# Normalization tile by tile in a fused seven-sublayer transformer kernel: x updated straight from PSUM, squares and sums placed among the products, h made and awaited per tile

## The reference

```python
h = x * rsqrt(mean(x * x, axis=-1) + 1e-6) * gain     # first block: h = h * (1 + scale) + shift
x = x + gate * sublayer(h)                            # second block: gate 1, no shift
```

## Time and profile before

| | us |
|---|---|
| median of 3 runs (range) | 3588.69 (3579.77 to 3588.9) |
| the profiled execution's own time | 3586.82 |
| its span, first to last instruction | 3584.4 |
| PE busy | 3003.4 (84%) |
| DVE busy | 2309.0 (64%) |
| ACT busy | 1371.9 (38%) |
| mean granted PE clock | 0.921 of full speed |

### The profile page before, as it was taken

One profiled execution on the slowest core, in us unless ns is written; L12 is line 12 of the kernel. 1 busy time (PEld: TensorE's weight loads), 2 busy tenths in 40 slices (PEclk: granted clock), 3 DMA queues, 4 the chain that ended last, 5 costly groups with the idle time before them and its releaser, 6 DMA issues.

```text
span 3584.4 us, 48021 instructions
## 1 busy us (share of the span) xinstructions
PE 3003.4 (84%) x18518; PEld 2646.4 (74%) x18518; DVE 2309.0 (64%) x3078; ACT 1371.9 (38%) x1347; POOL 498.3 (14%) x244
## 2 busy tenths in 40 slices
PE   1987537978986569855799999999877999999998
PEld 1776326867775558644699999888666999998887
DVE  5985555867645746445489787556554797874565
ACT  1433223434435134322344443444333444344443
POOL 0420001302200002000078100000000582000000
PEclk9999758989998789876899999999988999999999
DMA  6985204776543025420345566567543455665675
GB/s 232 344 277 177 78 0 147 268 241 229 205 158 117 0 98 185 152 71 1 132 166 184 200 217 216 189 240 283 203 141 111 166 181 189 224 221 188 238 275 201
DMA packets 146097, 640.20 MB, mean 179 GB/s; under 512 B 12057, under 2 KB 45889, under 8 KB 89409
## 3 DMA queue, kind: packets, MB, share of 16 engines
q1 hardware_dynamic: 127584, 572.12, 46.2%
q10 hardware_dynamic: 18400, 66.59, 5.1%
HBM read 604.04 MB, written 34.62 MB: 178 GB/s over the span
## 4 chain that ended last, share of the span: by engine, by line
PE 75%; DVE 14%; ACT 4%; DMA 4%; issue 3%; POOL 0%; DVEq 0%; SPq 0%; ACTq 0%
PE pp L436 19%; PE pp L438 10%; PE pp L547 7%; PE pp L548 7%; PE pp L549 7%; PE mz L614 6%; PE mz L616 6%; PE mz L617 6%; PE mz L590 2%; DVE ada_raw L1017 2%; PE mz L428 2%; DVE gsq L1078 2%; DMA ada_raw<-ada 1%; DVE w_lo L988 1%; ACT w_hi L737 1%
## 5 line engine op out<-in xcount | busy, mean ns | idle before, releaser
L988 DVE TENSOR_TENSOR w_lo<-raw,w_hi 128x2048 fp32r<-128x2048 f32 (+1 forms) x422 | 923.9, 2190 | 482.3 <-ACT w_hi L737 481.4
L737 ACT ACTIVATE w_hi<-raw 128x2048 fp32r<-128x2048 f32 (+1 forms) x486 | 894.5, 1841 | 511.2 <-DMA raw<-expert_v 366.1
L436 PE MATMUL pp<-hs,w_hi 128*128 128x512 f32 x2400 | 863.0, 404 | 123.2 <-DVE hs L1037 116.7
L438 PE MATMUL pp<-hs,w_lo 128*128 128x256 f32 x2400 | 678.5, 283 | 0.0
L436 PEld LDWEIGHTS pp<-hs,w_hi 128*128 128x128 f32 x2400 | 459.1, 191 | 243.6 <-DVE hs L1037 120.7
L547 PE MATMUL pp<-hs,w_hi 128*128 128x256 f32 x2048 | 584.8, 286 | 0.0
L548 PE MATMUL pp<-hs,w_hi 128*128 128x256 f32 x2048 | 579.3, 283 | 0.0
L549 PE MATMUL pp<-hs,w_lo 128*128 128x256 f32 x2048 | 579.1, 283 | 0.0
L1506 POOL TENSOR_TENSOR w_lo<-raw,w_hi 128x2048 fp32r<-128x2048 f32 x64 | 319.2, 4999 | 1224.3 <-ACT w_hi L737 1224.3
L438 PEld LDWEIGHTS pp<-hs,w_lo 128*128 128x128 f32 x2400 | 461.1, 192 | 0.0
L436 PE MATMUL pp<-us,w_hi 128*128 128x512 f32 x960 | 351.8, 409 | 107.2 <-DVE us L1089 74.5
(11 more groups left out here) (245 smaller groups left out, 3219.9 us busy)
## 6 DMA issues: line engine op xcount, KB each, us to landing
raw<-expert_u SPq DMA_DIRECT2D x128, 1024.0 KB, 4.9
raw<-expert_v SPq DMA_DIRECT2D x128, 1024.0 KB, 4.9
raw<-ffn_in SPq DMA_DIRECT2D x88, 1024.0 KB, 4.9
raw<-ffn_down SPq DMA_DIRECT2D x64, 704.0 KB, 4.1
ada_raw<-ada ACTq DMA_DIRECT2D x76, 512.0 KB, 5.4
ada_raw<-ada ACTq DMA_DIRECT2D x22, 1024.0 KB, 6.3
raw<-out_w SPq DMA_DIRECT2D x16, 1024.0 KB, 4.9
raw<-hgrn SPq DMA_DIRECT2D x16, 1024.0 KB, 4.9
```

Of the source, the lines that this page charges most:

```text
L436: mm(outp, w_hi[:, slot, a:a + P], rhs[:, k0 + k].rearrange("p a t -> p (a t)"), start=(k0 + k == 0), stop=False, skip_group_check=True)
L438: last = mm(outp[:, 0:T], w_lo[:, slot, a:a + P], rhs[:, k0 + k, 0, :], start=False, stop=(k0 + k == last_k), skip_group_check=True)
L737: f(w_hi[:, slot, 0:n], raw[:, slot, 0:n], ACT.Copy).then_inc(hi_ready, 1)
L988: v.tensor_tensor(w_lo[:, slot, 0:n], raw[:, slot, 0:n], w_hi[:, slot, 0:n].bitcast(F32), ALU.subtract)\
```

## The change

- **x from PSUM.** `ffn_down` and `out_product` have no cross copy and no `add_halves`. DVE does two multiply-adds per tile straight from PSUM (first half, a wait on itself, second half), and `x_done` counts tiles (8 per sublayer). PE waits for `x_done` where it waited for `evac_done`.
- **Squares and sums among the products.** ACT squares one or two tiles as soon as they are updated, from within its `ffn_down` and `out_product` loops; PE's sums stand between products. After `ffn_down` rows, seven of the eight sums stand before or within the last row; in `out_product`, two after the third chunk and two after the fourth.
- **Root.** ACT does a one-column Sqrt before the last squares, so that a table load falls there.
- **h per tile.** DVE computes `x * gain * inv_rms` per tile, ACT makes the high part with the shift as bias, DVE the low part; PE waits per tile in the first output tile of the next phase.
- **u per tile.** PE waits for 11 tiles of u at the first `ffn_down` product and then per tile.
- **After PEER.** `y_tok` is copied by ACT and DVE in four parts, transposes release x two tiles at a time, x is added in four steps. The output goes out in four transfers.
- `h32` moves to where `cross` and `both` lie, `sq` to a free region; ACT's wait for `hs_ready` (L783) goes, and so does its wait for `ada_read` before the first norm (L914).

```diff
@@ memory
+        h32 = at("h32", [P, KD, T], F32, M)
+        sq = at("sq", [P, KD, T], F32, B)
@@ SP
-            sp.wait_ge(x_done, NORMS)
-            sp.dma_start(out, xT[:]).then_inc(out_done, 16)
+            for b in range(4):
+                sp.wait_ge(x_done, KD * (NORMS - 1) + 2 * b + 2)
+                sp.dma_start(out[:, 2 * b:2 * b + 2], xT[:, 2 * b:2 * b + 2]).then_inc(out_done, 16)
@@ PE
+            def sums(n, a, b):
+
+                for k in range(a, b):
+                    pe.wait_ge(norm_sq, KD * n + k + 1)
+                    last = mm(mz[:, 0, 0:T], ones, sq[:, k, :], start=(k == 0), stop=(k == KD - 1), skip_group_check=True)
+                if b == KD:
+                    last.then_inc(norm_sum, 1)
...
+                def tile_of_h(k):
+                    pe.wait_ge(hs_ready, KD * n + k + 1)
...
-                pe.wait_ge(u_lo, KF * (q + 1))
                 pe.wait_ge(evac_done, ph.evac0)
-                for rp, pair, half, lap in pairs_of(pe, ph):
-                    pe.wait_ge(evac_done, ph.evac0 + rp - 1)
+
+                def tile_of_u(k):
+                    if k == 0 or k >= KF // 2:
+                        pe.wait_ge(u_lo, KF * q + max(k + 1, KF // 2))
+
+                for rp, pair, half, lap in itertools.chain(pairs_of(pe, ph.part(0, 2)), pairs_of(pe, ph.part(2, KD - 2))):
+                    if not isinstance(rp, int) or rp > 1:
+                        pe.wait_ge(x_done, KD * n + rp - 1)
                     for j in range(2):
                         pe.wait_ge(lo_ready, 2 * pair + j + 1)
+                        first = isinstance(rp, int) and rp == 0
+                        if isinstance(rp, int) and rp == KD - 1:
+                            sums(n + 1, *((0, 6), (6, 7))[j])
...
+                sums(n + 1, KD - 1, KD)
@@ PE out_product
+                        if c > 1:
+                            pe.wait_ge(x_done, KD * n + 2 * c - 2)
+                        for t in range(2):
+                            last = tile_product(pp[:, j, t], 2 * half + j, t * KD, us, 0, KD, KD - 1)
+                        last.then_inc(w_used, 1)
+                        if c > 1:
+                            sums(n + 1, 2 * c - 4, 2 * c - 2)
+                sums(n + 1, KD - 4, KD)
@@ ACT
+            def squares(n, a, w):
+
+                act.wait_ge(x_done, KD * (n - 1) + a + w) if n else act.wait_ge(x_in, 16)
+                f(sq[:, bass.ds(a, w)], xT[:, bass.ds(a, w)], ACT.Square).then_inc(norm_sq, w)
+
+            def norm(n, a):
+
+                f(small[:, 63:64], eps, ACT.Sqrt)
+                for k in range(a, KD, 2):
+                    squares(n, k, min(2, KD - k))
                 act.wait_ge(norm_sum, n + 1)
                 f(inv_rms[:], mz[:, 0, 0:T], ACT.Sqrt, bias=eps, scale=1.0 / D).then_inc(norm_rms, 1)
-                act.wait_ge(norm_h, n + 1)
-                f(hs[:, :, 0, :], h32[:], ACT.Copy).then_inc(norm_hi, 1)
-                if n in (0, 2, 3):
-                    act.wait_ge(hs_ready, n + 1)
+                for k in range(KD):
+                    act.wait_ge(norm_h, KD * n + k + 1)
+                    f(hs[:, k, 0, :], h32[:, k], ACT.Identity, bias=a_add[:, n, k:k + 1]).then_inc(norm_hi, 1)
@@ ACT ffn_down
                     for j in range(2):
                         split_next(ph, rp, pair, half, lap, j)
                         load_modulation(ph, 2 * rp + j + 1, 1 - j)
-                    take_cross(ph, ph.evac0 + rp, half, 2 * pair + 2, 1)
+                        if j == 0 and not (isinstance(rp, int) and rp == 0):
+                            squares(n + 1, rp - 1, 1)
@@ DVE
-                link(v.tensor_tensor(h32[:], xT[:], inv_rms[:].unsqueeze(1).to_broadcast([P, KD, T]), ALU.mult))
-                for k in range(KD):
-                    last = v.tensor_scalar(h32[:, k], h32[:, k], a_mul[:, n, k:k + 1], a_add[:, n, k:k + 1], ALU.mult, ALU.add)
-                last.then_inc(norm_h, 1)
-                dve.wait_ge(norm_hi, n + 1)
-                v.tensor_tensor(hs[:, :, 1, :], h32[:], hs[:, :, 0, :].bitcast(F32), ALU.subtract).then_inc(hs_ready, 1)
+                for k in range(KD + 1):
+                    if k < KD:
+                        v.scalar_tensor_tensor(h32[:, k], xT[:, k], a_mul[:, n, k:k + 1], inv_rms[:], ALU.mult, ALU.mult).then_inc(norm_h, 1)
+                    if k:
+                        dve.wait_ge(norm_hi, KD * n + k)
+                        v.scalar_tensor_tensor(hs[:, k - 1, 1, :], h32[:, k - 1], a_add[:, n, k - 1:k],
+                                               hs[:, k - 1, 0, :].bitcast(F32), ALU.add, ALU.subtract).then_inc(hs_ready, 1)
+
+            def add_to_x(ps, g, xk, done):
+
+                v.scalar_tensor_tensor(xk, ps[0], g, xk, ALU.mult, ALU.add).then_inc(x_half, 1)
+                dve.wait_ge(x_half, done + 1)
+                v.scalar_tensor_tensor(xk, ps[1], g, xk, ALU.mult, ALU.add).then_inc(x_done, 1)
@@ DVE after PEER
-                dve.wait_ge(y_mm, l + 1)
-                v.tensor_tensor(xT[:].rearrange("p k t -> p (k t)"), xT[:].rearrange("p k t -> p (k t)"),
-                                pp.rearrange("p a b n -> p (a b n)"), ALU.add).then_inc(x_done, 1)
+                dve.wait_ge(w_used, 2 * (ph.pair0 + ph.pairs))
+                for dh in range(2):
+                    v.tensor_copy(y_tok[:, 1, dh * 512:(dh + 1) * 512], mz[:, 2 + dh]).then_inc(y_cp1, 1)
+                for b in range(4):
+                    dve.wait_ge(y_mm, 4 * l + b + 1)
+                    xb_ = xT[:, 2 * b:2 * b + 2].rearrange("p k t -> p (k t)")
+                    v.tensor_tensor(xb_, xb_, pp[:, b // 2, b % 2], ALU.add).then_inc(x_done, 2)
```

More of the change, by code:

```diff
@@ L17 @@
+import itertools
 import math
@@ L528, in attention, with out_product @@
                 weigh(HEADS - 1)
-            def out_product(i):
+            def out_product(i, n):
                 pe.wait_ge(mix_lo, i + 1)
-                products(plan[("out", i)], us)
+                ph = plan[("out", i)]
+                for rp, pair, half, lap in each_pair(ph):
+                    for j in range(2):
+                        c = 2 * rp + j
+                        pe.wait_ge(lo_ready, 2 * pair + j + 1)
+                        if c > 1:
[6 more added lines that the diff above has]
+                sums(n + 1, KD - 4, KD)
             def up(ph, q, spread=None, fresh=False):
@@ L631, in _ @@
             pe.wait_ge(evac_done, 1)
[L633 to L635 removed]
+            sums(0, 0, KD)
+            ffn(0, 0)
             ph = plan[("attn", 0)]
[L637 removed]
+            products(ph, 1)
             pe.wait_ge(evac_done, ph.evac0 + ph.evacs)
@@ L913, in _ @@
             split(0, 0, 0, CHUNK)
-            act.wait_ge(ada_read, MOD_STEPS)
-            norm(0)
-            ffn(0)
-            norm(1)
+            squares(0, 0, KD)
+            norm(0, KD)
+            ffn(0, 0)
+            norm(1, KD - 1)
             ph = plan[("attn", 0)]
@@ L933, in _ @@
             split_mix(0, pj[:, 0:KD])
-            products(plan[("out", 0)])
-            norm(2)
-            ffn(1)
-            norm(3)
-            ffn(2)
-            norm(4)
+            out_product(0, 1)
+            norm(2, KD - 2)
+            ffn(1, 2)
+            norm(3, KD - 1)
+            ffn(2, 3)
+            norm(4, KD - 1)
             ph = plan[("hgrn", 0)]
@@ L958, in _ @@
             split_mix(1, pj[:, 0:KD])
-            products(plan[("out", 1)])
-            norm(5)
-            ffn(3)
-            norm(6)
+            out_product(1, 4)
+            norm(5, KD - 2)
+            ffn(3, 5)
+            norm(6, KD - 1)
             ph = plan[("swa", 0)]
@@ L1056, in ffn @@
                         modulation(ph, rp, j)
-                    add_halves(both[:, half, 0:1], e, half, 1)
-                    dve.wait_ge(evac_done, e + 1)
-                    xk = xT[:, bass.ds(rp, 1), :]
-                    last = v.scalar_tensor_tensor(xk, both[:, half, 0:1], a_gate[:, n, bass.ds(rp, 1)], xk, ALU.mult, ALU.add)
-                last.then_inc(x_done, 1)
+                    dve.wait_ge(w_used, 2 * pair + 2)
+                    add_to_x([pp[:, half, 0:1, a * T:(a + 1) * T] for a in range(2)], a_gate[:, n, bass.ds(rp, 1)],
+                             xT[:, bass.ds(rp, 1), :], KD * halves_of[n] + rp)
             def out_product(i, n):
@@ L1066, in out_product @@
                     for j in range(2):
-                        e = ph.evac0 + 2 * rp + j
-                        add_halves(both[:, j], e, j)
                         split_next(ph, rp, pair, half, j)
-                        dve.wait_ge(evac_done, e + 1)
+                        dve.wait_ge(w_used, 2 * pair + j + 1)
                         for t in range(2):
                             k = 4 * rp + 2 * j + t
-                            last = v.scalar_tensor_tensor(xT[:, k], both[:, j, t], a_gate[:, n, k:k + 1], xT[:, k], ALU.mult, ALU.add)
-                last.then_inc(x_done, 1)
```

(2 more changed lines are left out.)

120 lines of the change are left out of this document (60 added, 60 removed).

## The result

The changed kernel takes 3427.81 us (median of 4 runs, 3424.75 to 3428.49) against 3588.64 of the kernel before (4 runs): ratio 0.9556, 95% interval 0.9539 to 0.9572. The profiled execution took 3427.76, its span is 3426.0, 158.4 less than before.

A forecast was written before the change was run, and what follows sets the result against it. PE, busy 84% of the span, bounds the kernel, so gains come from its idle or slow time. 42 + 19 + 30 + 10 + 23 = 124 us off 3586.8, plus 1.9 to the median, gave 3464 us; range 3432 to 3495.

The forecast's parts named there:

- Part 1: Root to first finished output tile, ten norms: making h per tile overlaps DVE, ACT and PE; gain 42 us.
- Some slow pairs move behind it: First products after a norm: PE under half busy, so slow-clock pairs shift behind the eighth tile; 0.7 us lost per norm.
- 3 for norm 0: Root to first finished tile at norm 0: gain only 3 us, as its next stage runs with busy DVE and DMA.
- Rival B: PE's shorter rests keep it at the higher clock; 7 us more in Part 1, about 3444 us; chance 0.15.
- Parts 2 and 5: Behind ffn_down, squares and sums moved among products gain 19 us; PE's earlier start on u gains 23 us.
- there I count half: u gain in the first two ffn_down stages halved for DMA shares 0.96 and 0.90: 23 us, full value 29.
- rival A: Memory stream takes gains back in the first 816 us: half gives 3479 us, all 3494; sign: w_lo waits; chance 0.2.
- The last row's stall: Last ffn_down row's second half waits for tile 6's square behind ACT's split; a hold over 2 us would be wrong.
- Part 3: Behind out_product (norms 2, 5, 7, 9): squares and sums among products shorten PE's idle time; gain 30 us.
- Part 4: Behind the PEER layers, before norm 8 and at the end: split copies, adds and output transfers; gain 10 us.
- Rival D: ffn_down row loop through PE, DVE and ACT closes at 12 us a row, eating the gain: 3601 us; chance 0.02.
- Rival C: Per-tile handoffs between DVE and ACT don't overlap: 1.46 us per tile, 3501 us, half of it 3482; chance 0.07.

The follow-up runs named there:

- order_hl: Changed kernel with DVE finishing each tile of h (h, wait for ACT, low part) before beginning the next: 3491.55 us, ratio 0.9742.
- h_wide: Changed kernel with the norm's h made in wide steps, as before the change: 3492.19 us, ratio 0.9732.
- u_all: Changed kernel with PE again waiting for all 22 tiles of u before the first ffn_down product: 3461.03 us, ratio 0.9647.
- sums_after: Changed kernel with all eight sums behind the last ffn_down product: 3422.37 us, ratio 0.9548; repeated as sums_after_5: 3422.07 us, ratio 0.955.
- row_wait: Changed kernel with ACT waiting at each ffn_down row's end until PE finished the row: 3426.53 us, ratio 0.9561.
- after_again: The changed kernel, unaltered, run once more as a control in a later set: 3425.32 us, ratio 0.9568.

## Why the prediction was wrong

Direction, mechanism and the place of each gain were right; two sizes were too small. The 158.4 us of span, by the phases of the table above (a norm's share is its gap and what follows while h is short; a phase's own length is set apart):

| step (rounded) | forecast | measured |
|---|---|---|
| 1, root to first finished tile | 42 | 63 |
| 2 and 5, behind ffn_down, and u | 42 | 56 |
| 3, behind out_product | 30 | 33 |
| 4, PEER and the end | 10 | 8 |
| what else differs | 0 | -1 |

**Part 1 is the step that failed most.** "With one wait per tile I take 0.93 per tile": measured 0.79, twice the 0.40 of the earlier trace rows. The wait for ACT costs nothing in DVE's steady state, since ACT has answered, by 0.16 us in norm 1, when DVE comes to the low part; order_hl shows that it costs in another order. Seven tiles by 0.14 are 1.0 us per norm. "Some slow pairs move behind it ... I take 0.7": measured 0 to 0.2 in nine norms. The reason given for it, PE "under half busy", took 0.35 us per pair; PE was still at the lower clock there, where its own row has 0.64, and the window shows it busy for 3.19 of 3.20 us. In norm 1, 5.9 us pass from the first product to the ninth pair (290.61 to 296.50) and the pairs behind it are at the higher clock; before it was 4.4. In the mean of nine norms the gain is 7.6 of gap less 1.3 of stretch, 6.3, against 4.3; most of the last 0.3 of the difference is that the first pairs of the kernel before took 4.65 in the mean, not 4.4. "3 for norm 0" measured 6.1 up to the ninth pair, with 0.7 lost behind it: DVE's other work didn't stand in the way.

Rival B had the condition wrong and part of its price right. PE's shorter rests did not keep it at the higher clock: in norms 1 to 9 of the changed kernel's trace its first product ran at 0.50. But its 7 us in part 1 came nearly whole, since the slow pairs that the forecast put behind the eighth tile did not appear.

The Trainium skill ("VectorE: DVE Perf Modes", "The DRAIN you can't avoid") reports that eight copies with a semaphore after each took as long as with one after the last; the low parts above agree, 0.40 from start to start with a semaphore raised by each and a wait, already met, ahead of each, as between the two of the earlier trace rows, which have no wait between them. Its advice of 512 elements or more ("The TRN2 errata"), weighed in the prediction, did not decide: the part brought 63 us, and DVE is busy 6.3 us less than with the wide steps of h_wide. DVE's busy time as a whole rose by 4.2 us, where the prediction had it fall slightly.

**Parts 2 and 5: "there I count half".** The first two feed-forwards gave 13.3 and 17.3 us where I forecast 7.5 and 10, the other two 12.2 and 13.0 against 11.6 and 12. So 13.1 of the 14 us missed are where I let the stream take back, from DMA shares of 0.96 and 0.90. The halving itself makes 6.8 of them. Most of the rest is the last x, which came 2.4 and 3.9 us earlier against the stage's first product, where the forecast had 1.5 later and no change. (Added up from its own terms the forecast of parts 2 and 5 is 41, not 42.) u_all shows each of the four u waits worth 7 to 8 us. The waits for the low part of the weights that I named as the sign of rival A add up to nothing on PE in these stages of the changed kernel, and to 1.4 us at most in its second trace, u_all and sums_after. A high share in a window said that the queues were busy, not that PE was short of weights. Before the change, what those two stages ended with was DVE's list, as in the changed kernel, with waits for modulation tiles of 0.48 and 1.00 us in its last row: the last x lay 6.65 and 9.10 us behind the last product, now 2.93 and 2.91. Why the second came 3.9 us earlier against the stage's first product isn't settled: row_wait excludes ACT's wait as the cause, and the same kernel had 69.6 us in one trace and 72.1 in the other, so a good part may be scatter.

**The last row's stall** was foreseen and is small: in the second ffn_down PE waits 1.14 us for tile 6's square (1.4 in after_again), under the 2 us named as a sign, and in the others not at all. Sums within the stream cost 0.44 each, as forecast.

**Part 3** was right: behind out_product PE's gap is 7.9 to 9.6 us instead of 24.4 to 25.9. The table load ahead of norm 7's last square is there, and its gap is 1.7 longer:

```profile
1610.46 1.28 ACT L813 ACT_TABLE_LOAD   x1 [6.10 <-DVE xT L1094]
1611.75 0.20 ACT L813 ACTIVATE small<-small 128x1 f32<-128x1 f32 x1
1611.86 0.61 ACT L809 ACTIVATE sq<-xT 128x512 f32<-128x512 f32 x1
```

No table load stands at the Identities. The Trainium skill ("ScalarE: Activation LUTs", "Table sets: the hidden batching unit") had it so, and the trace agrees. **Part 4** came 2 us short. **Rival D** never came near: PE waits in no middle row of ffn_down in the changed kernel. **Rival C** was real as a mechanism; only DVE's order keeps it away, at 67 us.

## What to carry to other kernels

Split a long chain between engines by tile and put the next tile's first step ahead of the wait for the last one: here the interleaving was worth 67 us, and without it the split by tile gained nothing over the wide steps (3491.55 us against 3492.19). Before counting a gain as taken back by the memory, look for a wait of the bound engine on a transfer or its result in that stage; a high DMA share alone is no such wait. And read the list of the engine that makes the last input in program order: the work ahead of it (a 2.3 us weight split that PE needed only with its 17th pair, some 16 us later) was here what ended the stage.

## What was not expected of the hardware

PE's pairs of products run at one of two paces, 0.3467 or 0.3533 us from pair to pair, with the granted clock at 1.00 in both. The pace mostly holds for a whole phase and changes from run to run with the same code. Windows on PE within the third ffn_in, sums_after_5 and then after_again:

```profile
800.00:840.00 40.00, 40.00 (x229) 1.00 0.76 280
840.00:878.00 38.00, 38.00 (x217) 1.00 0.71 256
```

```profile
800.00:840.00 40.00, 40.00 (x233) 1.00 0.78 288
840.00:878.00 38.00, 38.00 (x221) 1.00 0.74 263
```

The same 40 us hold 229 products or 233. A phase of 125.2 us then takes 127.5, and the fourth ffn_in went from 123.9 before to 127.6 after the change, of which the thinner start makes only 1.3. What sets the pace stays open. It moves a whole run by several us, of the 4 to 14 between the runs of one kernel (an estimate: 2.3 us for each phase of 352 pairs), and so a difference of a few us between two traces is read from gaps, or from phases that ran at the same pace.
